# Attention values as the stationary operand of their product, with probabilities in two rounded parts, on one Trainium2 core

## The reference, cut to what matters

```python
def block(args):                                  # 16 blocks of 128 queries
    rel = relu(einsum('bthd,bsd->btsh', qib, ki)) # the indexer: 8 heads of 64
    iscore = einsum('btsh,bth->bts', rel, wib)    # one score for each key
    iscore = where(causal, iscore, -inf)
    _, idx = top_k(iscore, 256)                   # 256 keys are kept for each query
    ...
    s = einsum('btgrd,btkgd->btgrk', qg, ksel) * 64 ** -0.5
    p = softmax(where(valid, s, -inf))
    o = einsum('btgrk,btkgd->btgrd', p, vsel)     # the product that is changed
```

## Time and profile before

| | us |
|---|---|
| median of 3 runs (lowest to highest) | 3363.38 (3362.57 to 3368.68) |
| the profiled execution, own time | 3364.6 |
| its span, first to last instruction | 3362.8 |

### The profile page before, as it was taken

The page is one execution under the profiler, slowest core; times in us unless marked ns, Lnnn a source line. Parts: engine busy times, 40 slices in busy tenths (PEclk is TensorE's granted clock), DMA queues, the critical chain, the costliest instruction groups (busy, mean ns, idle before and its releaser), DMA issues.

```text
span 3362.8 us, 46208 instructions
## 1 busy us (share of the span) xinstructions
PE 3198.6 (95%) x17928; PEld 2822.9 (84%) x17928; DVE 2020.8 (60%) x3427; ACT 1284.1 (38%) x2117; POOL 237.1 (7%) x400
## 2 busy tenths in 40 slices
PE   8999999999889899999889999998999999989998
PEld 7999999998777788878778888887888888868886
DVE  4467778788566776666676555567855653341223
ACT  3454445455466454444443333335433332210000
POOL 0001000000111110000110001011100000010000
PEclk9999999999899899999999999999999999989999
DMA  5543343443323556565643343345333333465554
GB/s 183 163 129 133 132 142 113 132 133 123 115 86 127 187 203 225 212 227 217 244 152 128 134 142 140 129 162 200 125 125 125 123 116 126 154 242 195 175 211 165
DMA packets 167658, 529.15 MB, mean 157 GB/s; under 512 B 17296, under 2 KB 38160, under 8 KB 165392
## 3 DMA queue, kind: packets, MB, share of 16 engines
q1 hardware_dynamic: 165136, 522.00, 44.9%
q10 hardware_dynamic: 2304, 4.20, 0.3%
HBM read 393.41 MB, written 132.71 MB: 156 GB/s over the span
## 4 chain that ended last, share of the span: by engine, by line
PE 58%; DVE 6%; DMA 5%; ACT 2%; issue 2%; SPq 0%; DVEq 0%; POOL 0%; ACTq 0%; POOLq 0%
PE PJ_d L2130 8%; PE PJ_d L2132 8%; PE PJ_d L2131 8%; PE SC L2083 6%; PE PJ_d L2155 6%; PE PJ_d L2157 6%; PE PJ_d L2156 6%; PE SA L2042 3%; PE SA L2069 3%; PE SA L2043 3%; DMA split_d<-wd 3%; DVE score L1773 1%; DVE prob L1867 1%; DVE h_lo L1887 1%; ACT h_hi L1645 1%
## 5 line engine op out<-in xcount | busy, mean ns | idle before, releaser
L2130 PE MATMUL PJ_d<-h_hi,wd 128*128 128x512 f32 (+1 forms) x1472 | 577.1, 392 | 12.7 <-DVE h_lo L1887 8.3
L2132 PE MATMUL PJ_d<-h_hi,wd 128*128 128x512 f32 (+1 forms) x1472 | 565.2, 384 | 0.0
L2131 PE MATMUL PJ_d<-h_lo,wd 128*128 128x512 f32 (+1 forms) x1472 | 564.2, 383 | 0.0
L733 PE MATMUL PJ<-w_hi,h_hi 128*128 128x338 f32 (+1 forms) x1280 | 416.9, 326 | 2.7 <-DVE w_lo L550 2.7
L734 PE MATMUL PJ<-w_lo,h_hi 128*128 128x338 f32 (+1 forms) x1280 | 409.4, 320 | 0.0
L735 PE MATMUL PJ<-w_hi,h_lo 128*128 128x338 f32 (+1 forms) x1280 | 409.3, 320 | 0.0
L1867 DVE CUSTOM_DVE_ANT_0 prob<-SA,bias 128x1024 f32<-128x1024 f32 (+7 forms) x192 | 170.0, 911 | 354.1 <-PE SA L2043 350.6
L1627 ACT ACTIVATE pT<-SA 128x512 f32<-128x512 f32 (+3 forms) x320 | 156.4, 531 | 571.5 <-PE SA L2069 571.5
L2130 PEld LDWEIGHTS PJ_d<-h_hi,wd 128*128 128x128 f32 x1472 | 281.5, 191 | 63.2 <-DVE wd L1882 5.2
L2132 PEld LDWEIGHTS PJ_d<-h_hi,wd 128*128 128x128 f32 x1472 | 280.8, 191 | 54.6
L2131 PEld LDWEIGHTS PJ_d<-h_lo,wd 128*128 128x128 f32 x1472 | 281.7, 191 | 49.0
(11 more groups left out here) (207 smaller groups left out, 5600.6 us busy)
## 6 DMA issues: line engine op xcount, KB each, us to landing
wd<-split_d SPq DMA_DIRECT2D x420, 512.0 KB, 3.8
split_d<-wd SPq DMA_DIRECT2D x140, 512.0 KB, 4.6
w_raw<-in_w_in SPq DMA_DIRECT2D x40, 684.0 KB, 4.5
w_raw<-in_w_in SPq DMA_DIRECT2D x40, 676.0 KB, 4.5
wd_land<-in_w_gu SPq DMA_DIRECT2D x88, 256.0 KB, 3.3
row_h<-proj_d SPq DMA_DIRECT2D x16, 1024.0 KB, 7.1
proj_d<-stage SPq DMA_DIRECT2D x40, 342.0 KB, 4.5
proj_d<-stage SPq DMA_DIRECT2D x40, 338.0 KB, 5.1
```

The source lines that it names most:

```text
L733: t.matmul(out, h_hi[:, k, tok], w_hi[:, u, e], start=(k == 0), stop=False)
L2130: t.matmul(to[:, tok], w_hi[:, r, w], h_hi[:, c, tok], start=(c == 0 and part != 1), stop=False)
L2131: t.matmul(to[:, tok], w_hi[:, r, w], h_lo[:, c, tok], start=False, stop=False)
L2132: last = t.matmul(to[:, tok], w_lo[:, r, w], h_hi[:, c, tok], start=False, stop=(c == KD - 1 and part != 0))
```

## The change

In blocks 0 to 3 the arithmetic stays, with tiles of its own (`pT_early`, `V_early`). In blocks 4 to 15:

- POOL rounds each block's values and keeps the rest (`split_values`), high and low part side by side for each key/value head; SP stores them to `v_d` and loads them again for each block and each of the two heads (`load_values`, up to four transfers of 256 KB).
- ACT writes the rounded transposed probabilities beside room for the low part; DVE writes the low part (`turned_probs_low`). `values` waits for it.
- For each 128 keys there is one fp32r product: weights are the values' two parts (128 x 128), 256 columns of probabilities stream (high, low). The result stands transposed in SC[:, 0:256], 64 rows for each part of the values, 128 columns for each part of the probabilities.
- ACT copies one half of that out (`copy_low_output`), DVE adds the other (`add_output`), PE multiplies by a folded identity (`turn_output`, float32, 64 columns), which adds the values' parts and turns them back; for each two heads DVE divides (`attention_pair`) and SP stores.
- DVE's list: low part of the first pair, slot "B", low part of the second pair, and then the search parts "A" and "B" (before: search "A", slot "B", search "B"). With one pair: low part, search "A", slot "B", search "B".
- The projected rows come in two transfers and one place (`load_rest`, `load_q`) instead of one transfer and two places; POOL's work is cut in two likewise.

The core of the diff:

```diff
-            def prep(b):
-                turned_rows(g, pool, link, kept, kept.rt, b)
...
+            def split_values(b):
+                raw = row_of(b)[:, V0:V0 + KV * HD].rearrange("p (g d) -> p g d", d=HD)
+                if b >= 1:
+                    pool.wait_ge(v_stored, 16 * b)
+                link(g.tensor_copy(v_stage[:, :, 0, :], raw))
+                g.tensor_tensor(v_stage[:, :, 1, :], raw, v_stage[:, :, 0, :].bitcast(F32), ALU.subtract).then_inc(v_staged, 1)
...
+            def load_values(b, g):
+                sp.wait_ge(v_stored, 16 * (b + 1))
...
+                for c in range(NCH(b)):
+                    if v_before[b, g, c]:
+                        sp.wait_ge(pv_done, v_before[b, g, c])
+                    last = min(4 * c + 4, b + 1)
+                    sp.dma_start(v_tiles[c][:, 0:last - 4 * c, :].bitcast(F32), v_d[g, :, 4 * c:last, :]).then_inc(v_loaded[b, g, c][0], 16)
...
+            def copy_low_output(b, h):
+                n = late_no(b, h)
+                act.wait_ge(pv_done, pt_order[b, h, NCH(b) - 1] + 1)
+                if n >= 1:
+                    act.wait_ge(ot_turned, n)
+                s_.activation(oT[:], SC[:, P:2 * P], ACT.Copy).then_inc(ot_half, 1)
...
+            def turned_probs_low(b, h, p):
+                for c in range(2 * p, min(2 * p + 2, NCH(b))):
...
+                    dve.wait_ge(pt_ready, m + 1)
...
+                    v.tensor_tensor(to[:, :, 1, :], heads(of, w // P), to[:, :, 0, :].bitcast(F32), ALU.subtract).then_inc(pt_low, 1)
...
+            def add_output(b, h):
+                dve.wait_ge(ot_half, late_no(b, h) + 1)
+                v.tensor_tensor(oT[:], SC[:, 0:P], oT[:], ALU.add).then_inc(ot_ready, 1)
+            def attention_pair(b, j):
+                n = late_no(b, 2 * j)
+                dve.wait_ge(ot_turned, n + 2)
...
 (DVE's list)
                     if h + 1 < HEADS:
                         scores(b, h + 1)
+                    if not early(b) and h >= 1:
+                        add_output(b, h - 1)
...
                     fill(("A", b, h))
+                    for j in pairs_turned(b, h):
+                        attention_pair(b, j)
+                    if not early(b):
+                        turned_probs_low(b, h, 0)
+                    if pairs_of(b) == 2:
+                        fill(("B", b, h))
+                        turned_probs_low(b, h, 1)
                     for k in search(b, h, "A"):
                         topk_part(b + 1, k)
-                    fill(("B", b, h))
+                    if pairs_of(b) == 1:
+                        fill(("B", b, h))
                     for k in search(b, h, "B"):
                         topk_part(b + 1, k)
                     fill(("C", b, h))
...
 (PE's values)
-                    pe.wait_ge(pt_ready, m + 1)
+                    pe.wait_ge(pt_low, m + 1 - TS * HEADS)
+                    if h % GROUP == 0:
+                        pe.wait_ge(*v_loaded[b, g, c])
...
+                    if n >= 1 and c == 0:
+                        pe.wait_ge(ot_ready, n)
+                    if n >= 2 and c == 0:
+                        pe.wait_ge(att_ready, n // 2)
                     for kb in range(4 * c, min(4 * c + 4, b + 1)):
-                        last = t.matmul(SC[:, h * HD:(h + 1) * HD], pT[:, m % 2, (kb % 4) * P:(kb % 4 + 1) * P],
-                                        V[:, kb, g * HD:(g + 1) * HD], start=(kb == 0), stop=(kb == b))
+                        last = t.matmul(SC[:, 0:2 * P], values_of(kb), pT[:, m % 2, kb % 4].rearrange("p n t -> p (n t)"),
+                                        start=(kb == 0), stop=(kb == b))
+            def turn_output(b, h):
+                pe.wait_ge(ot_ready, n + 1)
...
+                t.matmul(SC[:, 2 * P + n % 2 * HD:2 * P + (n % 2 + 1) * HD], oT[:], folded, start=True, stop=True)\
+                 .then_inc(ot_turned, 1)
...
                     for p in range(pairs_of(b)):
                         turn_probs(b, h, p)
+                        if p == 0 and h >= 1:
+                            turn_output(b, h - 1)
                         fill(("BC"[p], b, h))
                         values(b, h, p)
```

More of the change, by code:

```diff
@@ L1115, in mixer_phase @@
         iota_ready = sem("iota_ready")
-        rows_ready, value0_ready = sem("rows_ready"), sem("value0_ready")
+        rest_in, q_in = sem("rest_in"), sem("q_in")
+        rest_ready, q_ready = sem("rest_ready"), sem("q_ready")
+        value0_ready, v_staged, v_stored = sem("value0_ready"), sem("v_staged"), sem("v_stored")
+        v_in = [sem(f"v_in{n}") for n in range(4)]
+        folded_ready = sem("folded_ready")
         hi_out = sem("hi_out")
@@ L1483, in _ @@
                     load_mix(0, 3)
-                for c in range(pairs_of(b + 1) if 2 <= b + 1 < NB else 0):
+                if not early(b):
+                    load_values(b, 0)
+                for c in range(pairs_of(b + 1) if has_idx(b) else 0):
                     for h in range(IH):
                         fill(("i", b, c, h))
+                        if c == 0 and h == 1 and b > TS:
+                            store(b - 1, HEADS // 2 - 1)
                 fill(("s", b))
+                if b == NB - 1:
+                    store(b - 1, HEADS // 2 - 1)
                 for h in range(HEADS):
+                    if b == 0 and h == GROUP:
+                        store_values(1)
+                    if not early(b) and h == GROUP:
+                        load_values(b, 1)
                     if h == HEADS - 2:
@@ L1492, in _ @@
                         fill((name, b, h))
-            store(NB - 1)
+                    for j in pairs_turned(b, h):
+                        store(b, j)
+            after(TAIL[0])
+            store(NB - 1, HEADS // 2 - 1)
             load_mix(NS - 1, 3)
-            for n in range(*TAIL):
+            for n in range(TAIL[0] + 1, TAIL[1]):
                 after(n)
@@ L1991, in _ @@
                     dve.wait_ge(iota_ready, 1)
-                if b >= 1:
-                    attention_half(b - 1)
-                for c in range(pairs_of(b + 1) if 2 <= b + 1 < NB else 0):
+                if 1 <= b <= TS:
+                    attention_early(b - 1)
+                if b > TS:
+                    add_output(b - 1, HEADS - 1)
+                    dve.wait_ge(bias_ready, b + 1)
+                for c in range(pairs_of(b + 1) if has_idx(b) else 0):
                     for h in range(IH):
@@ L2013, in _ @@
                     fill(("C", b, h))
-            attention_half(NB - 1)
-            for n in range(TAIL[0], LAST_STEP):
+            add_output(NB - 1, HEADS - 1)
+            step(TAIL[0])
+            attention_pair(NB - 1, HEADS // 2 - 1)
+            for n in range(TAIL[0] + 1, LAST_STEP):
                 step(n)
@@ L2071, in turn_probs, with values_early @@
                 last.then_inc(sa_full, 1)
+            def values_early(b, h):
+                g, m = h // GROUP, pt_order[b, h, 0]
+                pe.wait_ge(pt_ready, m + 1)
+                if m == 0:
+                    pe.wait_ge(value0_ready, 1)
+                if b >= 1 and h == 0:
+                    pe.wait_ge(att_early, b)
+                for kb in range(b + 1):
+                    last = t.matmul(SC[:, h * HD:(h + 1) * HD], pT_early[:, m % 2, kb * P:(kb + 1) * P],
+                                    V_early[:, kb, g * HD:(g + 1) * HD], start=(kb == 0), stop=(kb == b))
+                last.then_inc(pv_done, 1)
@@ L2173, in _ @@
                             fill(("i", b, c, h))
+                            if c == 0 and h == 1 and b > TS:
+                                turn_output(b - 1, HEADS - 1)
                 wait_pair_read(pe, use["keys", b])
@@ L2195, in _ @@
                         turn_probs(b, h, p)
+                        if p == 0 and h >= 1:
+                            turn_output(b, h - 1)
                         fill(("BC"[p], b, h))
                         values(b, h, p)
-            for n in range(*TAIL):
+            item(TAIL[0])
+            turn_output(NB - 1, HEADS - 1)
+            for n in range(TAIL[0] + 1, TAIL[1]):
                 item(n)
```

240 lines of the change are left out of this document (167 added, 73 removed).

## The result

| | before | after |
|---|---|---|
| median, us (lowest to highest) | 3362.98 (3354.33 to 3368.68) | 3431.93 (3427.18 to 3436.14) |
| runs | 4 | 4 |
| span of the profiled execution, us | 3362.8 | 3425.4 |
| mean granted clock of PE, share of full | 0.984 | 0.974 |

The change costs 2.1%: the ratio is 1.0207 (95% interval 1.0179 to 1.0234), 69 us by the medians; the two profiled executions, on which all that follows rests, differ by 62.6. The forecast was 3332 us in a range of 3285 to 3385; it has the wrong sign, and the range doesn't hold the time.

What follows compares the result with a forecast made beforehand. PE was taken to bound the kernel, except blocks 4, 8 and 12, where DVE set much of the pace. From 3364.6 us profiled, -67.0 + 26 + 10 = -31.0 gave 3333.6, as a median 3332; range 3285 to 3385.

Steps and rivals of the forecast that it cites:

- Blocks 4, 8 and 12: DVE sets much of the pace there; change in these blocks taken as +10 us, bounds -17.7 and +50.
- PE's gain: Blocks 4 to 15: cheaper fp32r products in `values`, less `turn_output`, net 84.8 us: 17.7 in blocks 4, 8, 12, 67.0 elsewhere.
- the rival in which loads aren't overlapped: PE's `values`: each product costs 0.226 us because its weight load isn't hidden; 3396 us, chance 0.03.
- The 8.6 us for leaving float32 less often: PE behind `values`: 0.09 us saved for each of 96 heads, as fp32r work now follows fp32r work.
- DVE's prices: DVE, blocks 4 to 15: low parts 178.6 us, `add_output` 28.0, `attention_pair` 23.5, `attention_half` -10.7; sum 219 us.
- That is the reserve on which the change draws.: DVE's 326.8 us of waits for PE's scores, in 76 places, were taken as room for the added DVE work.
- 26 us of new waits outside blocks 4, 8 and 12: PE waiting for DVE: 5.1 us for block 13, 8.6 for 14, 3 each for 9-11, 1 each for 5-7.
- The other block starts: Outside block 15's start, `turn_output` stands behind two indexer products and only the items' banks run short: 1.5 us.
- The search sets the pace: Rival: DVE's search fits less between low parts and `turn_output`, +80 us waits, +50 in blocks 4, 8, 12; 3426, chance 0.17.
- All hidden: Rival: DVE's reserve absorbs all added work, in blocks 4, 8 and 12 too; 3279 us, chance 0.14 with nearly all hidden.
- What costs nothing: ACT's copies, `add_output`'s wait for them, POOL's splits, SP's transfers: zero; values' transfers up to 24 x 2 us.

Runs made afterwards that it cites:

- b1_before_parked: Kernel before, blocks 4 to 15, with only two DVE waits for ACT's pT added and the search placed behind them, no added work: 3408.1 us, ratio 1.0128.
- e6_low_by_act: Changed kernel, but ACT writes the low parts, as zeros, and DVE has no low-part steps or waits for them; result less exact: 3338.4 us, ratio 0.9927.
- e3_low_parts_cut: Changed kernel, but DVE writes low parts in full only for head 0, one column otherwise; instructions and waits kept, result not exact: 3408.5 us, ratio 1.0139.
- e8_act_low_old_order: e6_low_by_act with search and slots in DVE's order from before the change, and the last head's turn_output later: 3332.3 us, ratio 0.9911.
- e9_high_only: e8_act_low_old_order without any low parts: 128-column products, no add_output, ACT copies the output; result less exact, fastest kernel of the study: 3309.9 us, ratio 0.9846.
- e7_search_ahead_of_A: Changed kernel with search parts "A" moved between the next head's scores and slot "A", part 11 counted to search "B": 3410.4 us, ratio 1.0145.

## Why the prediction was wrong, point by point

**The difference taken apart.** Going from the fastest kernel to after, one thing at a time: low parts by ACT, the wider product and the addition, +22 (3309.9 to 3332.3); DVE's order and the early turned output, +6 (3338.4); DVE has the low-part steps in its list, waiting, with little work, +70 (3408.5); their work, +23 (3431.9). The +70 holds DVE's waits, 59 us of small steps, and PE's dependence on a DVE that is behind; `b1_before_parked` puts a price of 46 us on the waits with the order behind them, in the other kernel. How the rest divides was not measured.

**The miss by the forecast's own terms.** The forecast had -31.0 us, the profiled executions +62.6, so 93.6 are to be explained. Blocks 4, 8 and 12: +44.5 instead of +10, 34.5 of the miss. The nine others: +25.2 instead of -41; there PE's gain is 15.6 short, the waits 23.3 over, and up to 27.3 are clock, which had no term. The rest of the kernel took 7.1 off. The largest terms are DVE's gaps in blocks 4, 8 and 12 counted as room, the clock, and the waits elsewhere.

**PE's gain.** Right in its prices. Timeline of PE in after, block 13:

```profile
2545.80 0.64 PE L2283 MATMUL SC<-pT,V 128*128 128x256 f32 x4
2546.28 0.64 PE L2283 MATMUL SC<-pT,values 128*128 128x256 f32 x4
2546.76 0.82 PE L2253 MATMUL SA<-ident,prob 128*128 128x128 f32 x6
```

Four products with four weight loads take 0.48 us, 0.12 each, where 0.119 was forecast; the rival in which loads aren't overlapped is out. The Trainium skill, "TensorE: Matmul & The Clock Gate", Part 3, lets a weight load overlap a running matmul only when the row groups differ; these loads take all rows and are hidden, so the trace disagrees with it. As a sum the gain came out at about 72 us where 84.8 was forecast (20 against 17.7 in blocks 4, 8 and 12, 51 against 67 elsewhere), by the table above and with its uncertainty. Mean distances from start to start at full clock, blocks 4 to 15, tell the same: 128 keys took 0.212 us before and 0.122 after, 91 us less (96.8 in the forecast), and `turn_output` took 17 (20.6). The 8.6 us for leaving float32 less often don't show as a sum: the first pass of the scores and indexer products took 0.211 us instead of 0.222, some 6 us less, but a transposition of probabilities took 0.107 instead of 0.100, some 7 more. What made these longer is open; stalls shorter than a matmul's modelled length hide in such means.

**DVE's prices.** Right. A low part of 512 columns takes 0.686 us against 0.687, of 128 columns 0.284 against 0.285, `add_output` 0.287 against 0.292, and by shape the whole sums to 210 us against 219. Groups by shape, DVE, of after:

```profile
L2020 DVE TENSOR_TENSOR pT<-SA,pT 128x512 fp32r<-128x512 f32 x216 | 141.5, 686 | 185.2 <-ACT pT L1754 185.0
...
L2033 DVE TENSOR_TENSOR oT<-SC,oT 128x128 f32<-128x128 f32 x96 | 27.5, 287 | 60.0 <-ACT oT L1762 59.6
```

The right half of the lines is what the forecast took for free: the low parts of 512 columns take 141.5 us and DVE stands 185.2 us in front of them.

**"That is the reserve on which the change draws."** This is the step that failed. The 326.8 us of the earlier trace rows were waits at one place, the scores, with everything else already done. The forecast saw that the search is queued behind the low parts, but it counted DVE's idle time as room all the same: by whole blocks in 4, 8 and 12, and in the other blocks by one stretch of one head, from the low parts to `add_output`. Its reading of the earlier trace rows was off the same way: DVE had 34 to 70% of blocks 5-7, 9-11, 13-14 and 15 free, not a fifth to two fifths. That time isn't there to be used: DVE reaches the low part when slot "A" is done, and then stands until PE has transposed and ACT has copied, once for each pair of chunks, with the search queued behind. Timeline of DVE, after, block 13, head 0:

```profile
2543.89 1.29 DVE L2020 TENSOR_TENSOR pT<-SA,pT 128x512 fp32r<-128x512 f32 x2 [2.49 <-ACT pT L1754]
...
2548.24 1.02 DVE L2020 TENSOR_TENSOR pT<-SA,pT 128x512 fp32r<-128x512 f32 x2 [3.06 <-ACT pT L1754]
2549.18 2.14 DVE L1958 TENSOR_REDUCE ends<-score 128x1 f32<-128x1920 f32 x1
...
2556.92 1.23 DVE L2006 CUSTOM_DVE_ANT_0 prob<-SA,bias 128x1024 f32<-128x1024 f32 x1
```

It stands 2.49 and 3.06 us, then searches, and reaches the next scores late, with no wait before them (in the earlier trace rows, block 14, it still had 4.17 us to spare there). In this head that costs PE nothing yet: PE's next wait of more than 0.6 us is at 2618.3, behind head 4. The spare time is gone, and PE pays for it where more comes together. The proof that the holding is what costs is `b1_before_parked` (46 us with no work added) and `e6_low_by_act` beside `e3_low_parts_cut`, not this timeline.

**26 us of new waits outside blocks 4, 8 and 12.** PE's idle time grew there by 49 us, nearly twice that. The block that was worked out in full was nearly right: behind heads 0 and 6 of block 14 and at the start of block 15 PE waited 2.5, 3.6 and 4.7 us, where 2.0, 1.4 and 5 were forecast. What it took for the blocks not worked out, by scaling, was too small: idle time rose by 10.3 us in 5-7 and 16.0 in 9-11, where 3 and 9 were taken. PE's timeline of after:

```profile
2866.68 0.61 PE L2295 MATMUL SC<-xt,oT 128*128 128x64 f32 x2 [4.72 <-DVE oT L2033]
2867.06 0.77 PE L2341 MATMUL PJ_d<-h_hi,wd 128*128 128x512 f32 x1
2867.63 0.63 PE L2342 MATMUL PJ_d<-h_lo,wd 128*128 128x512 f32 x1
2868.06 0.63 PE L2343 MATMUL PJ_d<-h_hi,wd 128*128 128x512 f32 x1
...
2870.19 0.40 PE L2342 MATMUL PJ_d<-h_lo,wd 128*128 128x512 f32 x1
2870.43 0.40 PE L2343 MATMUL PJ_d<-h_hi,wd 128*128 128x512 f32 x1
```

The chain to it is the one of the forecast, in DVE's timeline: the last low part, part 11 of the search, an addition, `add_output`.

```profile
2857.16 1.16 DVE L2020 TENSOR_TENSOR pT<-SA,pT 128x512 fp32r<-128x512 f32 x2 [2.81 <-ACT pT L1754]
2858.24 2.29 DVE L1939 MAX8 top<-score 128x8 f32<-128x2048 f32 x1
...
2864.61 1.23 DVE L1991 TENSOR_SCALAR bias<-score 128x2048 bf16<-128x2048 f32 x1 [0.90 <-DVE left_int L1983]
2865.75 0.68 DVE L2086 TENSOR_TENSOR acc<-acc,PJ_d 128x512 f32<-128x512 f32 x1
2866.35 0.28 DVE L2033 TENSOR_TENSOR oT<-SC,oT 128x128 f32<-128x128 f32 x1
```

The other block starts weren't 1.5 us: the longest wait for the turned output was 6.7.

**The clock, a term that the sum didn't have.** The timeline above shows it. Behind the pause of 4.72 us the 512-column products start 0.57 and 0.43 us apart, at the end 0.24 (0.229 in the earlier trace rows): the granted clock is 0.50 from 2866.8 to 2870.2 us, the lower level of 1.2 GHz, and then that of 2.4 GHz again. In blocks outside 4, 8 and 12 the half-clock time rose from 3.4 to 58.0 us. A product at that level takes about twice as long (0.43 us against 0.229), so half of such time is lost: at most 27 us there and 12 in blocks 4, 8 and 12, up to 39 us of the miss. Not every pause does this: in blocks 9 to 11 the idle time rose from 5.9 to 21.9 us and the half-clock time from 0 to 6.8 only.

**Blocks 4, 8 and 12: +10.** They grew by 44.5 us (6.5, 22.8 and 15.2), just inside the bound of +50. But not in the way the bound was made: it had DVE at about 91, 87 and 95%, and by the windows DVE is at 81, 71 and 79%. DVE isn't full, it is held, five heads in a row with the search behind each low part: taking the work out of the low parts (`e3_low_parts_cut`) gave 4.4 us back there, taking the waits out as well (`e6_low_by_act`) 34.3. `e8_act_low_old_order` ran them at +4.4, +6.3 and -4.2 us against before.

**The rivals.** "The search sets the pace" gave 3426 and is the nearest by time. Its picture of a search that doesn't fit between the low parts and `add_output` is right, its sizes aren't: it had 80 us of waits outside blocks 4, 8 and 12 where there were 49 of idle and up to 27 of clock, and nothing of the clock. It had a chance of 0.17; the point against it, that reserve, was the wrong reading. "All hidden" needed DVE free, and even `e6_low_by_act` doesn't reach its 3279.

**What costs nothing.** Not all of it did. ACT's copy of the output was to be ready with several microseconds in hand; DVE stood 58.7 us in front of it, the third place at which it is held. The values' transfers landed in about 5 us each, but they stand in SP's queue behind the weights. That cost PE one wait: in block 5 `values` stood 4.09 us, for a releaser that the profile doesn't name, until a transfer issued at 1286.20 and landed at 1290.58.

```profile
1290.67 0.77 PE L2283 MATMUL SC<-pT,V 128*128 128x256 f32 x2 [4.09 <-issue]
```

```profile
1286.20 0.38 SPq L1394 DMA_DIRECT2D V<-v_d  x1
```

POOL gave PE no wait. The transfers by the page's DMA issues:

```profile
values<-v_d SPq DMA_DIRECT2D x30, 256.0 KB, 5.5
...
V<-v_d SPq DMA_DIRECT2D x24, 256.0 KB, 4.6
```

**What stays open.** Blocks 5 to 7 are 9 us longer than before even in `e8_act_low_old_order` (435.4 against 426.1), and 2.3 longer in `e9_high_only`. The wait for the values' transfer is there in both (5.1 and 4.5 us), so it is about half of the 9; how the rest divides wasn't isolated. It isn't shown either what holds the remaining 38 us of idle time in `e6_low_by_act`. A low part computed exactly by ACT or POOL wasn't tried.

## What to carry to other kernels

Don't count free time of an engine that works in order as a reserve for an instruction that itself waits on others: the engine stands there with the rest of its list behind it. So count for each new instruction how long it is held and what is queued behind, before counting its work. To see what the wait costs apart from the work, put the bare wait into the old kernel (here 46 us) and cut the work in the new one (here 23 of some 110 us). And where PE sets the pace, price a pause of a few microseconds at more than its length, since the clock can fall behind it.

## What the runs showed of the hardware that was not expected

Pauses of PE of a few us went with a lower clock in blocks that had hardly any: 3.4 us at half clock before and 58.0 after, with 20.6 and 70.0 us of idle. In the same blocks the other runs lie between: 17 at half clock with 36 of idle (`b1_before_parked`), 24 with 35 (`e6_low_by_act`), 41 with 62 (`e7_search_ahead_of_A`). No run varied the pauses alone. A tensor-tensor step of one column took 156 ns (`e3_low_parts_cut`) against 284 for 128 and 686 for 512, so cutting small DVE steps soon stops paying.
